# Sparse attention of a two-block transformer kernel: probabilities weighted before the transposes, values stationary, branches summed in PSUM

## The reference

```python
s_c = einsum('bghtd,bgnd->bghtn', qb, k_cmp) - slopes * (tf[:, None] - cmp_mid[None, :])
p_c = masked_softmax(s_c, cmp_end[None, :] <= t[:, None], -1)
o_c = einsum('bghtn,bgnd->bghtd', p_c, v_cmp)          # 15 compressed blocks
...
p_s = masked_softmax(s_s, mask_s, (-2, -1))            # 4 blocks of 64 keys, all selected at 256 tokens
o_s = einsum('bghtnl,bgtnld->bghtd', p_s, vg)
...
p_w = masked_softmax(s_w, mask_w, -1)                  # window of 512, so causal over 256 tokens
o_w = einsum('bghts,bgsd->bghtd', p_w, vwb)
return gb[..., 0:1] * o_c + gb[..., 1:2] * o_s + gb[..., 2:3] * o_w
...
g_a, g_b = split(sigmoid(z_gate), 2)
m = g_a * (o_a @ w_branch_rwkv) + g_b * (o_b @ w_branch_nsa)
```

## Time and profile before

| | |
|---|---|
| median of three runs | 1266.38 us (1266.21 to 1267.42) |
| the profiled execution | 1266.9 us |
| its span, first to last instruction | 1265.1 us |
| busy: PE, weight loads, DVE, ACT, POOL | 98%, 88%, 71%, 53%, 19% |
| granted clock of PE | 0.999 |
| weights and inputs read | 186.5 MB, 148 GB/s |

### The profile page before, as it was taken

The page is one execution under the profiler, slowest core; times in us unless marked ns, Lnnn a source line. Parts: engine busy times, 40 slices in busy tenths (PEclk is TensorE's granted clock), DMA queues, the critical chain, the costliest instruction groups (busy, mean ns, idle before and its releaser), DMA issues.

```text
span 1265.1 us, 26440 instructions
## 1 busy us (share of the span) xinstructions
PE 1235.9 (98%) x9988; PEld 1108.2 (88%) x9988; DVE 892.9 (71%) x1737; ACT 668.7 (53%) x1281; POOL 240.7 (19%) x358
## 2 busy tenths in 40 slices
PE   7999999999999999999999999999999999999997
PEld 6999999899989988999889977888888977888886
DVE  6778888756766767878746667777746866877744
ACT  5565555544367646666435467434435677443432
POOL 0112222231345202333303000121200100122100
PEclk9999999999999999999999999999999999999999
DMA  8321211115421354554555422545454633445552
GB/s 344 130 101 69 69 68 69 69 68 183 167 86 68 117 186 164 169 194 169 199 195 196 163 100 101 187 179 199 172 196 172 210 122 129 167 177 187 192 187 86
DMA packets 27058, 189.95 MB, mean 150 GB/s; under 512 B 2992, under 2 KB 3248, under 8 KB 4816
## 3 DMA queue, kind: packets, MB, share of 16 engines
q1 hardware_dynamic: 25920, 182.61, 40.2%
q0 software_dynamic: 1040, 5.96, 1.5%
HBM read 186.47 MB, written 1.05 MB: 148 GB/s over the span
## 4 chain that ended last, share of the span: by engine, by line
PE 91%; DVE 3%; ACT 3%; issue 1%; DVEq 1%; DMA 1%; POOLq 0%; POOL 0%; ACTq 0%; SPq 0%
PE ps L620 35%; PE ps L566 16%; PE ps L681 12%; PE ps L683 6%; PE ps L932 3%; PE ps L591 1%; PE ps L764 1%; PE ps L600 1%; PE ps L772 1%; PE ps L1033 1%; PE ps L949 1%; PE ps L1023 1%; PE ps L832 1%; ACT h_both L1521 1%; PE ps L1043 1%
## 5 line engine op out<-in xcount | busy, mean ns | idle before, releaser
L1543 ACT ACTIVATE w_hi<-ring 128x1024 fp32r<-128x1024 f32 x125 | 132.6, 1060 | 292.0 <-PE ps L620 152.8
L2116 DVE TENSOR_TENSOR w_lo<-ring,w_hi 128x1024 fp32r<-128x1024 f32 x125 | 155.4, 1243 | 129.4 <-ACT w_hi L1543 129.2
L681 PE MATMUL ps<-h_both,w_hi 128*128 128x512 f32 x672 | 237.7, 399 | 0.0
L683 PE MATMUL ps<-h_both,w_lo 128*128 128x256 f32 x672 | 188.7, 281 | 0.0
L620 PE MATMUL ps<-h_both,w_hi 128*128 128x256 f32 x912 | 165.7, 284 | 0.8 <-DVE w_lo L2122 0.8
L2122 DVE TENSOR_TENSOR w_lo<-ring,w_hi 128x1024 fp32r<-128x1024 f32 x125 | 157.8, 1262 | 0.0
L681 PEld LDWEIGHTS ps<-h_both,w_hi 128*128 128x128 f32 x672 | 126.3, 188 | 31.4
L566 PE MATMUL ps<-oT_r,ring_r 128*128 128x256 f32 x512 | 144.2, 282 | 0.0
L620 PEld LDWEIGHTS ps<-h_both,w_hi 128*128 128x128 f32 x912 | 142.5, 192 | 1.4 <-DVE w_lo L2122 1.2
L1548 ACT ACTIVATE w_hi<-ring 128x1024 fp32r<-128x1024 f32 x125 | 130.8, 1046 | 0.0
L620 PE MATMUL ps<-h_both,w_lo 128*128 128x256 f32 x456 | 129.0, 283 | 0.0
(11 more groups left out here) (441 smaller groups left out, 2869.9 us busy)
## 6 DMA issues: line engine op xcount, KB each, us to landing
ring<-in_weights SPq DMA_DIRECT2D x170, 1024.0 KB, 4.8
arena<-in_aux POOLq DMA_DIRECT2D x1, 2112.0 KB, 13.3
grow<-in_rows POOLq DMA_DIRECT2D x3, 512.0 KB, 4.8
cst<-in_consts SPq DMA_DIRECT2D x1, 1497.5 KB, 18.2
x<-in_x SPq DMA_DIRECT2D x2, 512.0 KB, 4.5
arena<-in_swbias POOLq DMA_DIRECT2D x1, 1024.0 KB, 10.5
arena<-arena POOLq DMA_DIRECT2D x1, 1024.0 KB, 12.7
out<-xn SPq DMA_DIRECT2D x4, 256.0 KB, 2.2
```

The source lines that it names most:

```text
L681: pe.matmul(bank[:].rearrange("p (a t) -> p a t", a=2), hi, h_both[:, :, k, :], start=k == 0, stop=False)
L683: m = pe.matmul(bank[:, 0:S], lo, h_hi[:, k, :], start=False, stop=k == KT - 1)
L1543: act.activation(w_hi[:, half_of(u0, m), WH:], ring[:, (u0 + m) % RING, WH:], ACT.Copy).then_inc(w_hi_p, 1)
L2116: dve.tensor_tensor(w_lo[:, half_of(u0, m), WH:], ring[:, (u0 + m) % RING, WH:], w_hi[:, half_of(u0, m), WH:].bitcast(F32), ALU.subtract). ...
```

## The change

The outputs of the three branches are no longer made in rows and transposed at the end. The probabilities are scaled first (gate over sum, per token), while they still lie in rows; then they are transposed, and the values stand still while the transposed probabilities stream past. The result is transposed from the start, and the three branches add up in one PSUM bank per pair of heads.

- In the compressed branch DVE scales the exponentials by gate over sum (`c_ready`) before PE transposes them, and makes the arguments of the next group only after that. The product moves into the attention: for each pair of heads one matmul with 128 columns of `Vblk` stationary (L593 of the new kernel).
- In the attention there are four buffers of probabilities and sums instead of two. DVE scales the probabilities in place (two `tensor_scalar`). Item `s-2` is transposed in step `s`, and items `s-4` and `s-3` are multiplied together at even `s`, as column tiles of 64 (L598).
- A pair of heads, finished after four items, is split by ACT (high) and DVE (low) right away into `o_hi` and `o_lo`. The 16 transposes of `o_rows` and the split behind them are gone.
- Keys of the two branches are stored without padding; the later biases, transposed compressed probabilities and `m_lo` have places of their own.
- ACT's `take_mixer(6)` comes in step 32, before its last two copies of transposes.

```diff
@@ PE attention
-                for s in range(N + 2):
+                for s in range(N + 3):
...
-                    if 1 <= s <= N:
-                        t = s - 1
+                    if s >= 4 and s % 2 == 0:
+                        t = s - 4
+                        pair, second = t // 4, t % 4 // 2
+                        o = ps[4 + pair % 2]
+                        if not second:
+                            if pair >= 2:
+                                pe.wait_ge(g_lo_ready, pair)
+                            g, cols = pair // 2, slice(pair % 2 * P, pair % 2 * P + P)
+                            pe.matmul(o[:, 0:S], Vblk[:, g, cols], cpT[:, g].rearrange("p b t -> p (b t)"),
+                                      start=True, stop=False)
+                        pe.wait_ge(pt_ready, n0 + t + 2)
+                        for kt, tokens, cols in ((0, slice(0, S), slice(0, S)), (1, slice(P, S), slice(S, KEYS))):
+                            for e in range(2):
+                                m = pe.matmul(o[e * HD:(e + 1) * HD, tokens], insts[t + e][2](kt), pT[:, e, cols],
+                                              start=False, stop=second == 1 and kt == 1)
+                        m.then_inc(o_mm, 1)
+                    if 2 <= s < N + 2:
+                        t = s - 2
                         pe.wait_ge(p_ready, n0 + t + 1)
...
-                    if s >= 2:
-                        t = s - 2
-                        values = insts[t][2]
...
-                        pe.matmul(o[:, 0:HD], pT[:, t % 2, 0:P], values(0), start=True, stop=True)
-                        pe.matmul(o[:, HD:2 * HD], pT[:, t % 2, P:2 * P], values(0), start=True, stop=False)
-                        pe.matmul(o[:, HD:2 * HD], pT[:, t % 2, 2 * P:3 * P], values(1), start=False,
-                                  stop=True).then_inc(o_mm, 1)
@@ PE compressed branch
-                pe.wait_ge(c_exp, g + 1)
+                for _ in range(3):
+                    next(dense)
+                pe.wait_ge(c_ready, g + 1)
+                if g:
+                    pe.wait_ge(c_pT, g)
...
-                m.then_inc(c_pv, 1)
-                next(dense)
+            pe.wait_ge(c_pT, GROUPS)
@@ ACT
+                    elif s == N:
+                        before(N)
+                    if 2 <= s < N + 2:
+                        t = s - 2
                         act.wait_ge(t_mm, n0 + t + 1)
...
+                    if s >= 7 and s % 4 == 3:
+                        pair = s // 4 - 1
+                        act.wait_ge(o_mm, n0 + 2 * pair + 2)
+                        act.activation(o_hi[:, pair, :], ps[4 + pair % 2][:, 0:S], ACT.Copy).then_inc(h_hi_ready, 1)
@@ DVE compressed branch
-                if g + 1 < GROUPS:
-                    cmp_args(g + 1)
...
+                dve.tensor_tensor(cp_[:, :, 0:N_CMP], cp_[:, :, 0:N_CMP],
+                                  cst8[:, 3, :].unsqueeze(2).broadcast_to((P, 8, N_CMP)), ALU.mult).then_inc(c_ready, 1)
+                if g + 1 < GROUPS:
+                    cmp_args(g + 1)
@@ DVE weigh
-                return dve.tensor_tensor(mx2[:, j, 2:4], mx2[:, j, 0:2], gate[:, :, g, 3 * hh + 1 + br], ALU.mult)
+                for b, cols in enumerate((slice(0, P), slice(P, KEYS))):
+                    ins = dve.tensor_scalar(p[:, cols], p[:, cols], m[:, 6 + b:7 + b],
+                                            gate[:, b, g, 3 * hh + 1 + br:3 * hh + 2 + br], ALU.mult, ALU.mult)
```

More of the change, by code:

```diff
@@ L219, in build @@
         qP = carve(PAIRS, S)
+        assert top[0] == 5 * UNIT, top[0]
         kcT, vcT = carve(GROUPS, S), carve(GROUPS, S)
-        ksP, kwP = carve(GROUPS, 2, S), carve(GROUPS, 2, S)
+        ks, kw = carve(GROUPS, S), carve(GROUPS, S)
+        late_biases = carve(2, KEYS)
+        cpT = carve(GROUPS, NB, P)
         v_sw = carve(NB, 512)
         blk = [carve(16, GROUPS * N_CMP), carve(16, GROUPS * N_CMP)]
-        hid = [carve(GROUPS * N_CMP) for _ in range(2)]
-        ga_, gb_ = carve(GROUPS * N_CMP), carve(GROUPS * N_CMP)
         xg = carve(2, GROUPS * N_CMP)
@@ L1187, in _ @@
                 m.then_inc(c_tr, 1)
-                for _ in range(2):
-                    next(dense)
-                pe.wait_ge(c_pT, g + 1)
-                for b in range(NB):
-                    m = pe.matmul(ps[2 + g % 2][:, b * S:(b + 1) * S], cpT[:, b, :], Vblk[:, g, :], start=True, stop=True)
-                m.then_inc(c_pv, 1)
-                next(dense)
+            pe.wait_ge(c_pT, GROUPS)
             half_rows = [slice(0, HD), slice(HD, P)]
             attention([(qP[half_rows[e], HPG // 2 * g + pair, :],
-                        (lambda lo, hi, g=g, e=e, k=(ksP, kwP)[br]: k[half_rows[e], g, e, lo:hi]),
+                        (lambda lo, hi, g=g, e=e, k=(ks, kw)[br]: k[half_rows[e], g, lo:hi]),
                         (lambda kt, g=g, br=br: v_sw.rearrange("p b (w g d) -> p b w g d", w=2, g=GROUPS)[:, kt, br, g, :]))
@@ L1204, in _ @@
                       NSA0, dense, mixer_pieces)
-            for _ in range(2):
-                next(dense, None)
-            transposes(o_rows)
             for _ in dense:
@@ L1530, in raw_boundary @@
                 act.activation(rstd_row, ps[7][:, 0:S], ACT.Copy).then_inc(xn_act, 1)
-            def split_rows_of_heads(hi):
-                n = n_norm["act"]
-                for q in range(4):
-                    act.wait_ge(tr_ready, 4 * n + q + 1)
-                    act.activation(flat(hi)[:, q * 512:(q + 1) * 512], ps[HEADS_T[q]][:],
-                                   ACT.Copy).then_inc(h_hi_ready, 1)
             def high_p(u0, m, i=0):
@@ L1853, in _ @@
                 act.wait_ge(c_tr, g + 1)
[L1854 removed]
+                act.activation(cpT[:, g].rearrange("p b t -> p (b t)"), ps[1][:, 0:S], ACT.Copy).then_inc(c_pT, 1)
                 if g == 0:
@@ L1994, in _, with attention, low_rows @@
             ps = list(banks)
-            def attention(N, n0, weigh, finish, between):
-                for s in range(N + 2):
+            def attention(N, n0, weigh, between):
+                def low_rows(pair):
+                    dve.wait_ge(h_hi_ready, pair + 1)
+                    dve.tensor_tensor(o_lo[:, pair, :], ps[4 + pair % 2][:, 0:S], o_hi[:, pair, :].bitcast(F32),
+                                      ALU.subtract).then_inc(g_lo_ready, 1)
+                for s in range(N + 1):
                     if s < N:
@@ L2584, in low_parts @@
                         lo.then_inc(oa_ready, 1)
[L2586 removed]
             gate = gates[:].rearrange("p b (g e) -> p b g e", g=GROUPS)
             def weigh(t):
[L2591 to L2592 removed]
+                g, hh, br = t // 8, t % 8 // 4 * 2 + t % 2, t % 4 // 2
+                m, p = sums[t % 4], masses[t % 4]
+                dve.reciprocal(m[:, 6:8], m[:, 4:6])
                 dve.drain()
[L2594 to L2606 removed]
+                for b, cols in enumerate((slice(0, P), slice(P, KEYS))):
+                    ins = dve.tensor_scalar(p[:, cols], p[:, cols], m[:, 6 + b:7 + b],
+                                            gate[:, b, g, 3 * hh + 1 + br:3 * hh + 2 + br], ALU.mult, ALU.mult)
+                return ins
+            attention(2 * H, NSA0, weigh, low_parts)
             split_one(ONE + 9)
```

129 lines of the change are left out of this document (42 added, 87 removed).

## The result

| | before | after |
|---|---|---|
| median of the runs compared | 1266.81 us (1266.21 to 1267.54) | 1272.44 us (1271.99 to 1273.20) |
| ratio | | 1.0044, interval 1.0034 to 1.0055 |
| profiled execution, span | 1266.9, 1265.1 us | 1273.2, 1271.3 us |

The change makes the kernel slower by 5.6 us. The forecast was 1265.3 us with a range up to 1269.5: wrong in sign and outside its range.

The account below looks back on a forecast made before the run. TensorE was taken to bound the kernel, at 91% of the last chain. PE's work -7.3, group-loop waits +4.6, ACT +1.4 and DVE +0.2 gave -1.1 us from the median 1266.38: 1265.3 us, range 1260.5 to 1269.5.

Parts of the forecast that it names:

- waits of the group loop: Compressed branch's loop over four groups: PE waits for scaled probabilities, arguments and the last copy; +4.6 us, ends 2.0 and 6.5.
- clock in the group loop: Group loop: granted clock stays at 1.00 behind the new holes, no loss; a fall was given 2 in 100.
- the rest of the loop: Group loop: the compressed branch's product leaves it, 3.4 us, and returns inside the attention.
- the attention, to the next stage: Attention: products 20.8 us out, 15.2 in, compressed products 3.4 in, transposes 1.7 out; ACT +1.4, DVE +0.2.
- everything behind it: Later stages: PE goes on with dense work, so the stage's shift reaches the end.
- TensorE's clock falls in the new holes: Rival, slower: clock falls behind new holes, put at 1.5 us at most; 2 in 100, within the slower case.
- this stretch (+0.5): Group loop: DVE's small operations stretch while POOL splits a unit, lengthening group 1's critical chain by 0.5 us.
- Next PE wants to overwrite the scores: Group loop: for group 3's scores PE waits 1.0 us until DVE has taken group 2's out for its arguments.
- ACT in the attention: Attention: mixer units delay copies, waits at step 25, step 11 and the end; +1.4 us, ends -0.9 and 4.
- PE's balance: PE's own work: old products and finished-row transposes out, paired products in; -7.3 us, bounds -5.5 and -9.
- DVE's pace: Rival, slower: between a double step's reductions, scalings beyond 1.25 us set the pace, 1270 us; 0.20 including longer waits.
- the term of +0.2: DVE in the attention: two in-place scalings an item, 0.55 us for both, 0.7 slack; ends 0 and +6.

Follow-up runs that it names:

- mixer_first: Changed kernel with ACT's first mixer unit right behind the exponentials of group 0 and its half weight unit behind those of group 3; 1266.94 us.
- The four kernels of the table above: Changed kernel with PE's three dense pieces ahead of or behind the group's transposes: scaled 1272.44 and 1271.48 us, compressed branch's scaling left out 1267.89 and 1263.77 us.
- even_steps: Changed kernel with ACT's mixer units at steps 12 and 26 instead of 11 and 25, two of the last four pieces ahead of the last products; 1270.25 us.
- unscaled_old_order: Changed kernel without the compressed branch's scaling, next arguments right behind the sum, PE's three dense pieces behind a group's transposes; a measurement only; 1263.77 us.
- best: mixer_first and even_steps, plus two pieces ahead of the next scores from group 1, five late idle products, a piece before the last-copy wait; 1261.09 us.
- exps_first: Changed kernel with ACT's first mixer unit behind the exponentials of group 1 and its half weight unit behind those of group 3; 1266.92 us.
- args_early: Changed kernel with DVE making the next group's arguments right behind the sum of exponentials, ahead of the scaling; 1273.91 us.
- old_order: Changed kernel, scaling included, with PE's three pieces of dense work behind a group's transposes again; 1271.48 us.
- idle_group: Changed kernel with products of no use ahead of group 1's transposes and of group 3's scores and transposes; 1269.95 us.
- idle_mla: Changed kernel with 16 products of no use in the last attention's wait near 1031 us; 1275.69 us.

## Why the prediction was wrong

Against the forecast shift of -1.1 us the span grew by 6.2. The 7.3 between them, by stretch:

| step of the prediction | forecast | measured | short by |
|---|---|---|---|
| waits of the group loop | 4.6 | 6.5 | 1.9 |
| clock in the group loop | 0 (2 in 100) | 2.7 | 2.7 |
| the rest of the loop | -3.4 (products gone) | -3.0 | 0.4 |
| the attention, to the next stage | -2.3 | -1.6 | 0.7 |
| everything behind it | 0 | +1.6 | 1.6 |

- **The step that failed is the rival "TensorE's clock falls in the new holes".** It rested on one row: a hole of the old kernel behind which the clock stayed at 1.00, and "my holes are 1.5 at most". Both halves were wrong. The holes were 2.0 and 1.65 us with 0.4 of work between them; in mixer_first the clock fell behind a single one of 1.5. And the hole of the earlier trace rows is no proof: the clock falls behind it in some executions and not in others. One execution that keeps its clock bounds nothing. The loop's fall alone is 2.7, the later one 1.3: 4.0 of the 7.3 us.
- **Without the clock the forecast would still have missed the sign.** 6.2 less 4.0 is +2.2 us, some 1268.6: inside the range, but slower and not faster. Most of that part is the size of the waits.
- **The waits of the loop: right places and releasers, size too small.** Four of four are where the prediction put them. Group 1's transposes were forecast at 1.5 + 0.5 and took 2.0 to 2.2. The scores of group 3 took 1.65 to 1.9 against 1.0, since DVE's operations beside POOL take 0.7 each: the prediction had added this stretch (+0.5) to one chain and not to the next, though the earlier trace rows show POOL at work for 5.6 us. The Trainium skill ("GPSIMD Engine Reference", section "Specifications") states that GpSimd shares its SBUF interfaces with VectorE, in contention with VectorE's instructions of two SBUF inputs or in a two-port mode. The trace agrees for L2547 and L2531, which have two SBUF inputs (0.28 alone, 0.72 beside POOL), and for L2523, which has one and stays at 0.27. L2529 has one tensor input and stretches all the same (0.17 to 0.68); whether it runs in a two-port mode no run here shows. Group 3's transposes waited 1.55 to 1.8 against 1.0.
- **The cause was more than the added wait.** The prediction named the exposed scores ("Next PE wants to overwrite the scores") but laid the blame on the order of DVE alone. The four kernels of the table above show that PE's own piece order costs up to 5.0 in the loop, 4.1 by the medians.
- **ACT in the attention: the working was right, the discount wrong.** The reckoning gave holes of 0.6, 1.4 and 1.0, together 3.0 - 0.9 = 2.1; the weight loads of the trace wait 0.7, 1.6 and 1.0, and even_steps, which removes these holes, takes 2.2 off. The forecast went down to 1.4 because the old kernel hid some of its units. Why the old kernel hid more is open. A reason that fits is that the products with the values now wait for both items of a pair; it was not tested apart.
- **PE's balance: right.** The double step is 4.08 with no compressed product and 4.51 with one (390.37 to 394.88 us), 4.3 on average as forecast; 4.41 - 1.30 + 0.95 is 4.06, and 0.43 for the product. That is 0.33 gained a step, as the rate of the earlier trace rows said, and not more. The rule of the Trainium skill ("TensorEngine Tiling (Array Packing)", section "Overview") gives up to twice the rate for a dimension of at most 64. An estimate by it is 4.41 - 0.65 = 3.8 for that step; the trace, with 4.08, does not reach it. unscaled_old_order and best, in which these savings reach the end, show them as a gain.
- **DVE's pace: no time lost, price wrong.** Its two scalings of an item take 1.03 us on average (32.8 us for 64), not 0.55 and above the end of 0.8 that was given. The 0.5 more is inside the 0.7 of slack that the rival worked out, and PE's weight load waited 0.3 us once: the term of +0.2 held by the slack and not by its price.

## What to carry to other kernels

Price a new hole of a busy TensorE twice: once as idle time, and once by the clock that may follow, whose loss here was 1.3 us for a fall of 3.4 and 2.7 for one of 6.8. Where a step makes an engine wait for a ring through two others, write down for each of the three queues what stands in the ring ahead of the critical instruction: moves of whole blocks (a mixer unit ahead of a copy, a half weight unit behind the last exponentials, pieces ahead of scores and of the last waits, units on even steps), with five idle products in a late hole, turned a loss of 5.6 us into a gain of 6.0 without touching the arithmetic. The idle products alone gave the kernel before nothing that can be told. A long piece of side work belongs where its engine is idle already, and its consumers' start has to be checked at the same time, as POOL's was not in exps_first.

## What the runs showed of the hardware

- The granted clock went to 0.50 behind holes of 1.5 to 4.1 us, single ones (mixer_first, args_early) or two close together, and stayed at 1.00 behind others of 1.6 (exps_first), 2.1 (the second of old_order) and 2.3 us (the kernel before). Falls lasted 3.4 us or twice that, with PE busy nearly throughout. With products of no use in the holes it stayed at 1.00 (idle_group in the loop, idle_mla near 1031 us).
- A product of plain f32 operands with 256 columns ran as two records, 0.44 us in all, against 0.12 for one of the split weights' products of the same size.
- Some of DVE's operations on 8 and 120 columns, 0.17 and 0.28 us alone, took 0.68 to 0.82 beside POOL. Others kept their length beside it: a sum over 120 columns always took 0.28.
